# The head of a hybrid streaming-encoder layer: first modulation in four groups of two channel blocks, x transposed in six banks

## What is computed

```python
c_act = jax.nn.silu(c)
mod = (c_act @ w_mod[l] + b_mod[l])[:, None, :]
sh_m, sc_m, gt_m, sh_f, sc_f, gt_f = jnp.split(mod, N_MOD, axis=-1)
h = rms_norm(x, g_pre_mix[l]) * (1.0 + sc_m) + sh_m
y = hybrid_mixer(h, w_in[l], ...)          # begins with proj = h @ w_in, 1024 x 7168
x = x + gt_m * rms_norm(y, g_post_mix[l])
h = rms_norm(x, g_pre_mlp[l]) * (1.0 + sc_f) + sh_f
y = sq_relu_mlp(h, w_mlp_up[l], w_mlp_down[l])
x = x + gt_f * rms_norm(y, g_post_mlp[l])
```

## Time and profile before

| | us |
|---|---|
| median of three executions | 836.4 |
| lowest, highest | 834.62, 836.66 |
| the profiled execution | 835.04 |
| its span in the profile | 833.3 |
| PE busy within the span | 813.3 |

### The profile page before, as it was taken

How to read it: one execution, slowest core, us unless ns; L and a number is a source line. 1 busy time by engine, 2 the same in 40 slices (tenths; PEclk the granted TensorE clock), 3 DMA queues, 4 the chain that set the end, 5 groups by cost and what they waited for, 6 DMA issues and landing times.

```text
span 833.3 us, 12458 instructions
## 1 busy us (share of the span) xinstructions
PE 813.3 (98%) x4270; PEld 701.9 (84%) x4270; DVE 507.5 (61%) x682; ACT 440.0 (53%) x650; POOL 28.3 (3%) x24
## 2 busy tenths in 40 slices
PE   6799999999999999999999999999999999999997
PEld 6588888888888888888888899999999888888885
DVE  4746677656685565566675579777777533333335
ACT  6356777766674444444334566676767622333332
POOL 1542000000000000000000000000000000000000
PEclk9899999999999999999999999999999999999999
DMA  9942333326077666667337031333333532223302
GB/s 290 348 130 82 107 108 107 107 82 182 26 210 219 181 197 201 189 177 209 129 101 253 1 101 44 109 102 101 101 101 101 177 101 96 85 96 101 101 0 101
DMA packets 134943, 109.52 MB, mean 131 GB/s; under 512 B 4460, under 2 KB 119300, under 8 KB 134916
## 3 DMA queue, kind: packets, MB, share of 16 engines
q1 hardware_dynamic: 134740, 109.10, 43.8%
q10 hardware_dynamic: 144, 0.04, 0.0%
q0 software_dynamic: 32, 0.02, 0.0%
HBM read 107.04 MB, written 2.10 MB: 131 GB/s over the span
## 4 chain that ended last, share of the span: by engine, by line
PE 97%; DVE 1%; ACT 1%; POOL 0%; issue 0%; DMA 0%; DVEq 0%; ACTq 0%
PE ps L416 32%; PE ps L417 31%; PE ps L418 31%; PE ps L1460 1%; PE ps L1471 0%; PE ps L1607 0%; PE ps L1483 0%; POOL ht_lo L600 0%; ACT xnt L657 0%; ACT ht_hi L659 0%; PE ps L1579 0%; PE ps L1580 0%; PE ps L1491 0%; DMA crows<-in_c_dram 0%; DVE sums L1331 0%
## 5 line engine op out<-in xcount | busy, mean ns | idle before, releaser
L416 PE MATMUL ps<-ht_hi,w_hi 128*128 128x512 f32 x448 | 176.9, 395 | 8.0 <-POOL ht_lo L600 5.2
L417 PE MATMUL ps<-ht_lo,w_hi 128*128 128x512 f32 x448 | 175.8, 392 | 0.0
L418 PE MATMUL ps<-ht_hi,w_lo 128*128 128x512 f32 x448 | 175.6, 392 | 0.0
L1020 DVE TENSOR_TENSOR w_lo<-raw,w_hi 128x1024 fp32r<-128x1024 f32 x100 | 122.0, 1224 | 56.7 <-ACT w_hi L630 54.9
L630 ACT ACTIVATE w_hi<-raw 128x1024 fp32r<-128x1024 f32 x96 | 100.4, 1049 | 33.3 <-PE ps L418 28.7
L416 PEld LDWEIGHTS ps<-ht_hi,w_hi 128*128 128x128 f32 x448 | 84.9, 189 | 27.2 <-issue 9.5
L418 PEld LDWEIGHTS ps<-ht_hi,w_lo 128*128 128x128 f32 x448 | 84.9, 190 | 18.0
L417 PEld LDWEIGHTS ps<-ht_lo,w_hi 128*128 128x128 f32 x448 | 85.1, 190 | 17.5
L416 PE MATMUL ps<-w_hi,hd_hi 128*128 128x512 f32 x256 | 99.6, 389 | 0.0
L417 PE MATMUL ps<-w_lo,hd_hi 128*128 128x512 f32 x256 | 99.6, 389 | 0.0
L418 PE MATMUL ps<-w_hi,hd_lo 128*128 128x512 f32 x256 | 99.6, 389 | 0.0
(11 more groups left out here) (227 smaller groups left out, 1492.9 us busy)
## 6 DMA issues: line engine op xcount, KB each, us to landing
raw<-in_w_in_dram SPq DMA_DIRECT2D x48, 512.0 KB, 4.8
modraw<-in_w_mod_dram SPq DMA_DIRECT2D x32, 512.0 KB, 4.0
raw<-in_w_mlp_down_dram SPq DMA_DIRECT2D x32, 512.0 KB, 3.3
up_raw<-in_w_mlp_up_dram SPq DMA_DIRECT2D x56, 256.0 KB, 3.4
mod_raw<-in_w_mod_dram SPq DMA_DIRECT2D x32, 256.0 KB, 7.0
xs<-in_x_dram SPq DMA_DIRECT2D x8, 512.0 KB, 5.3
raw<-in_w_a_out_dram SPq DMA_DIRECT2D x8, 512.0 KB, 5.4
raw<-in_w_b_out_dram SPq DMA_DIRECT2D x8, 512.0 KB, 5.5
```

What stands on the lines that cost most here:

```text
L416: nc.tensor.matmul(dst, l_hi, r_hi, start=first, stop=False, skip_group_check=chained)
L417: nc.tensor.matmul(dst, l_hi, r_lo, start=False, stop=False, skip_group_check=chained)
L418: return nc.tensor.matmul(dst, l_lo, r_hi, start=False, stop=last, skip_group_check=chained)
L1020: V.tensor_tensor(w_lo[:, slot, :], raw[:, slot, :], f(w_hi[:, slot, :]), ALU.subtract).then_inc(w_lo_ready, 1)
```

## The change

`GROUPS` becomes four pairs, so the first group covers blocks 0 and 1 and needs 2 MB of weights in place of 1 MB. In it PE takes rows 0 to 3 directly (`mod0_direct`, 16 matmuls of one column, between and behind the transposes), and DVE rows 4 to 7 in `ps`; PE adds DVE's sum with the ones vector. x is transposed into six banks; blocks 6 and 7 are transposed behind the others, into banks 4 and 5 once ACT has copied these to `xnt`. ACT modulates blocks 0 and 1 straight out of `ps`. The unread transposes between the tiles go, and 14 come to stand between the columns of group 0 and the first matmul block. The first weights are split per block instead of per group. SP issues all x tiles, then all eleven vector DMAs, then the modulation's chunks with a block's weights between them. ACT loads its tables for sigmoid and root by one-element activations ahead of need. The columns of the next group are made at (1,1), (3,1), (5,1). Every DVE accumulation of a group now stands behind the column step of the group before.

```diff
-    GROUPS = ((0,), (1,), (2, 3), (4, 5), (6, 7))
+    GROUPS = ((0, 1), (2, 3), (4, 5), (6, 7))
+    PE_ROWS = 4
...
-                    if g0 == 0 and m0 > 0:
-                        sp_eng.wait_ge(mod0_sum, 1)
+                    if g0 == 0 and m0 < PE_ROWS:
+                        sp_eng.wait_ge(mod0_rows, m0 + num0)
...
             for t in range(TB):
                 sp_eng.dma_start(xs[:, t, :], x_v[:, t, :]).then_inc(xr_in[t], 16)
-                if t == 0:
-                    load_vectors(sp_eng, vectors[1::2], vec_in)
-            load_mod0_group(0)
+            load_vectors(sp_eng, vectors, vec_in)
+            per_group = len(CHUNKS) // len(GROUPS)
+            for c in range(per_group):
+                load_mod0(c)
             load_first_units(0)
-            load_first_units(1)
...
+            for g in range(1, len(GROUPS)):
+                for i in range(per_group):
+                    load_mod0(g * per_group + i)
+                    if i == 1:
+                        load_first_units(GROUPS[g - 1][1])
+                    if i == 2:
+                        load_first_units(GROUPS[g][0])
+            load_first_units(NB - 1)
...
             first_units_lo(0)
             pool.wait_ge(h_lo, 1)
+            input_lo(1)
+            first_units_lo(1)
             for g in range(1, len(GROUPS)):
-                first_units_lo(g)
-                for k in GROUPS[g]:
-                    input_lo(k)
+                k0, k1 = GROUPS[g]
+                first_units_lo(k0)
+                input_lo(k0)
+                input_lo(k1)
+                first_units_lo(k1)
...
-            load_vectors(act, vectors[0::2], vec_in)
+            act.wait_ge(const_ready, 4)
+            A(ysum[:, 3 * TB - 1:3 * TB], eps_t[:, 0:1], ACT.Sigmoid)
             act.wait_ge(c_sum, 1)
             A(c_act[:, :], ps[:, B_T0, 0:NB], ACT.Sigmoid).then_inc(sig_c, 1)
+            A(ysum[:, 3 * TB - 2:3 * TB - 1], eps_t[:, 0:1], ACT.Sqrt)
...
-            act.wait_ge(x_tr, NB)
-            for k in (NB - 1, NB - 2, 0, 1, 2):
-                if k == 1:
-                    first_units_hi(0)
+            act.wait_ge(x_tr, X_BANKS)
+            for k in (4, 5, 2):
                 A(xnt[:, k, :], ps[:, k, :], ACT.Copy).then_inc(xnt_ready, 1)
-            act.wait_ge(xnt_ready, 5)
-            modulate(0, 0)
+            first_units_hi(0)
+            for k in GROUPS[0]:
+                modulate(k, 0)
+            first_units_hi(1)
...
-            accumulate(0, range(NB // 2))
-            dve.wait_ge(x_tr, NB)
-            for k in (3, 4, 5):
-                V.tensor_copy(xnt[:, k, :], ps[:, k, :]).then_inc(xnt_ready_dve, 1)
+            accumulate(0, range(PE_ROWS, NB))
+            dve.wait_ge(x_tr, X_BANKS)
+            V.tensor_copy(xnt[:, 3, :], ps[:, 3, :]).then_inc(xnt_ready_dve, 1)
             dve.wait_ge(cols_ready, 2)
             modulation_columns(0)
-            dve.wait_ge(xnt_ready, 2)
-            accumulate(1, range(0, 2))
+            dve.wait_ge(x_tr, NB - 1)
+            V.tensor_copy(xnt[:, 6, :], ps[:, X_LATE[6], :]).then_inc(xnt_ready_dve, 1)
             dve.wait_ge(h_hi, 1)
             V.tensor_tensor(ht_lo[:, 0, :], xnt[:, 0, :], f(ht_hi[:, 0, :]), ALU.subtract).then_inc(h_lo, 1)
-            accumulate(1, range(2, NB))
+            dve.wait_ge(x_tr, NB)
+            V.tensor_copy(xnt[:, 7, :], ps[:, X_LATE[7], :]).then_inc(xnt_ready_dve, 1)
             for g in range(1, len(GROUPS)):
-                if g + 1 < len(GROUPS):
-                    dve.wait_ge(mod0_acc, acc_count(g, NB - 1))
-                    accumulate(g + 1, range(0, 1))
+                accumulate(g, range(NB))
                 modulation_columns(g)
-                if g + 1 < len(GROUPS):
-                    accumulate(g + 1, range(1, NB))
...
+            def mod0_direct(blocks):
+                for m in blocks:
+                    c = CHUNK_OF[0, m]
+                    if m == CHUNKS[c][1]:
+                        pe.wait_ge(mod0_in[c], 32)
+                    for a in range(2):
+                        for k in GROUPS[0]:
+                            last = nc.tensor.matmul(ps[:, B_T1, a * NB + k:a * NB + k + 1],
+                                                    chunk_view(c)[:, m - CHUNKS[c][1], a, k * P:(k + 1) * P],
+                                                    c_act[:, m:m + 1], start=m + a + k == 0, stop=False, skip_group_check=True)
+                    last.then_inc(mod0_rows, 1)
...
-            COLUMNS_AT = {(0, 5): 1, (1, 5): 2, (3, 1): 3, (5, 1): 4}
+            COLUMNS_AT = {(1, 1): 1, (3, 1): 2, (5, 1): 3}
...
+                    if k == 0 and i == 1:
+                        pe.wait_ge(h_f32, 2)
+                    if k == 0 and i >= 3:
+                        pe.wait_ge(xnt_ready_dve, i - 2)
```

More of the change, by code:

```diff
@@ L250, in hybrid_layer_kernel @@
         xnt_ready_dve = sem("xnt_ready_dve")
+        mod0_rows = sem("mod0_rows")
         mod0_acc = sem("mod0_acc")
@@ L1067, in accumulate @@
                         dve.wait_ge(mod0_in[c % M0_BUFS], 32 * (c // M0_BUFS + 1))
[L1068 to L1069 removed]
+                    if m == (PE_ROWS if g == 0 else 0):
+                        V.tensor_scalar(acc, part, c_act[:, m:m + 1], None, ALU.mult).then_inc(mod0_acc, 1)
                     else:
@@ L1456, in _, with unread, mod0_columns @@
             nc.tensor.transpose(ps[:, B_T0, 0:NB], crows[:, :], ident[0:NB, 0:NB]).then_inc(c_sum, 1)
-            def unread(count):
+            def unread(count, dst):
                 for _ in range(count):
-                    nc.tensor.transpose(ps[:, NB // 2, (TB - 1) * P:], ident[:, :], ident[:, :])
-            unread(24)
-            pe.wait_ge(vec_in, 16 * len(vectors))
-            nc.tensor.transpose(ps[:, B_T1, 0:NCOL], vrows[0:NCOL, :], ident[0:NCOL, 0:NCOL]).then_inc(cols_sum, 1)
+                    nc.tensor.transpose(dst, ident[:, :], ident[:, :])
+            def mod0_direct(blocks):
[9 more added lines that the diff above has]
+                    last.then_inc(mod0_rows, 1)
+            def mod0_columns(g):
+                pe.wait_ge(mod0_acc, acc_count(g, NB - 1))
+                for k in GROUPS[g]:
+                    for a in range(2):
+                        last = nc.tensor.matmul(ps[:, B_T1, a * NB + k:a * NB + k + 1], mod0[:, a, k * P:(k + 1) * P],
+                                                ones[:, 0:1], start=g > 0, stop=True, skip_group_check=True)
+                last.then_inc(mod0_sum, 1)
+            last_tokens = ps[:, X_BANKS - 1, (TB - 1) * P:]
+            unread(24, last_tokens)
             pe.wait_ge(cact, 1)
@@ L1467, in _ @@
                 pe.wait_ge(x_norm, t + 1)
-                for k in range(NB):
-                    if t == 0 and k == B_T1:
-                        pe.wait_ge(cols_ready, 1)
+                for k in range(X_BANKS):
                     last = nc.tensor.transpose(ps[:, k, t * P:(t + 1) * P], xs[:, t, k * P:(k + 1) * P], ident[:, :])
@@ L1473, in _ @@
                         last.then_inc(x_tr, 1)
[L1474 to L1495 removed]
+                if t == 0:
+                    pe.wait_ge(vec_in, 16 * len(vectors))
+                    nc.tensor.transpose(ps[:, B_T0, P:P + NCOL], vrows[0:NCOL, :], ident[0:NCOL, 0:NCOL]).then_inc(cols_sum, 1)
+                if t == 1:
+                    mod0_direct(range(0, 2))
+            mod0_direct(range(2, PE_ROWS))
+            for k, late in X_LATE.items():
+                pe.wait_ge(xnt_ready, late - 3)
+                for t in range(TB):
+                    last = nc.tensor.transpose(ps[:, late, t * P:(t + 1) * P], xs[:, t, k * P:(k + 1) * P], ident[:, :])
+                last.then_inc(x_tr, 1)
             pe.wait_ge(const_ready, 3)
             mod0_columns(0)
[L1498 to L1501 removed]
+            pe.wait_ge(xnt_ready, 3)
+            unread(14, ps[:, 2, 0:P])
+            COLUMNS_AT = {(1, 1): 1, (3, 1): 2, (5, 1): 3}
             for k in range(NB):
[L1503 to L1504 removed]
+                pe.wait_ge(w0_lo_ready, k + 1)
                 pe.wait_ge(h_lo, k + 1)
```

98 lines of the change are left out of this document (33 added, 65 removed).

## The result

| | before | after |
|---|---|---|
| median, us | 836.4 | 840.54 |
| lowest, highest | 834.62, 836.66 | 838.71, 842.32 |
| the profiled execution | 835.04 | 840.54 |
| its span | 833.3 | 838.7 |
| mean granted clock in it | 0.992 | 0.987 |

Each kernel was executed five times. The ratio after to before is 1.0058, with a 95% interval of [1.0037, 1.0078]. The forecast of 827.7 and its range up to 831.7 were wrong, in size and in sign.

What follows compares the result with a forecast made beforehand. PE, busy 98%, was taken as the bound: the first block would end at 20.1 + 38.3 = 58.4 against 66.43, 8.0 us less, giving 827.0 from the profiled execution or 828.4 from the median; 827.7 was taken, range 825.0 to 831.7.

Steps and rivals of the forecast that it cites:

- cost nothing as long as x's own 2.1 MB cover them: In the head: moving the eleven vector loads to SP, 3.6 us of issue ahead of the modulation, costs no time.
- rival of a late vector: In the head: a late vector or chunk stops PE; 832.4 us, or 829.5 with half the delay; chance 8%.
- S: Start of the first matmul block, forecast at 20.1 us, bounds 19.4 to 22.0.
- S + 38.3: Forecast end of the first matmul block, counted from its start S; 58.4 us against 66.43 before.
- The data of group 0: In the head: x, vectors and the first group's weights, 4.26 MB, are in at 14.7 us, bounds 13.7 to 15.2.
- rows 6 and 7, 0.81 us each: In the head: once the data are in, DVE does these two rows and is done at 16.3 us.
- since with the clock at full the sum closes: In the head: the reason given for keeping S at 20.1 us, within bounds of 19.4 to 22.0.
- The rival had the right places: Clock falls ahead of the block (1.5 us) or after (1,1) (nine matmuls, 1.8 us); 829.2 to 831.0 us; chance 30%.
- The 0.22 us of a transpose at half clock: In PE's head: 20 transposes at half clock would add 2.2 us, up to 1.5 to 1.9 on S.
- 0.8 ... 0.94 of slack, so nothing: Hand-over behind the block: ACT and DVE come 0.8 us later against PE, within 0.94 of slack at `g_lo`, costing nothing.
- given back behind the block: Hand-over slack is used up and DVE trails PE in the next units; 833 to 836 us; chance 5%.
- slower: Clock stays at half through the block; gain gone from 40 of 144 matmuls, 55 give 838 us; chance 4%.

Runs made afterwards that it cites:

- a2: The changed kernel with the vectors issued as before, five on SP behind x tile 0 and six on ACT; 835.8 us, ratio 1.0001.
- c3: c1 with DVE's first row of pair 2-3 put ahead of block 0's low part; 831.03 us, ratio 0.9932.
- d3: c3 with 14 unread transposes in front of the columns at (1,1); 833.28 us, ratio 0.9952.
- c2: c1 with 34 unread transposes ahead of the first x tile in place of 24; 832.65 us, ratio 0.996.
- d1: c3 with six unread transposes behind each of tiles 0 to 2 and each of the first two direct rows; 832.16 us, ratio 0.996.
- d2: d4 with d1's unread transposes in the head; 831.77 us, ratio 0.9955.
- a1: The changed kernel with POOL's memset of modb two units later; 833.15 us, ratio 0.9944.
- c4: The changed kernel with its last softplus steps written in two-tensor form, four for three, memset in place; 836.06 us, ratio 0.9981.
- c1: The changed kernel with both a1's later memset and a2's vector order; 831.26 us, ratio 0.9927.
- d4: a2 with c3's row, d3's filling and the softplus moved ahead of the columns of pair 4-5; 831.35 us, ratio 0.9945.

## Why the prediction was wrong

**The vectors (step: "cost nothing as long as x's own 2.1 MB cover them").** Wrong, and its rival of a late vector, given 8%, is what happened: the last vector released PE at 11.46. I counted bytes (0.06 MB) and issue time (3.6 us beside x), not what eleven small transfers do to the queues: 270 GB/s where a2 had 357, and a first chunk issued at 6.8 where a2 had 4.3. No run separates these two. The block began 4.9 us later than forecast; 3.5 of it is this (a2: 21.54). Of the 3.5, 1.1 is the vectors' transpose itself (11.46 against 10.39); the other 2.4 came up between it and the ones matmuls (9.77 us against 7.33), where after is at half clock from 12.0 to 18.5 and a2 only to 12.3. By the rival's own sum the end of the block would be S + 38.3 = 63.3.

**The data of group 0 (14.7, and "rows 6 and 7, 0.81 us each").** Mis-sized even without the vectors: in a2 DVE starts its four rows at 13.89 and has them done at 17.1, not 16.3. The third chunk was late and DVE had all four rows still to do, not two. In c3 the columns ended at 18.23 (17.21 + 1.02), not 17.2, and the block began 2.87 later, 2.9 forecast: so rows and columns are the last microsecond of S (21.10).

**The clock ("since with the clock at full the sum closes").** The rival had the right places, ahead of the block and behind (1,1), but in after the stretch behind (1,1) holds 15 matmuls, not nine: 3.0 us, which is about the difference between S + 38.3 and 66.33 - 25.04 = 41.3. In d3, where it does not fall, the block ends 38.1 behind its start (21.46 to 59.5, against 58.4 forecast; the end is the gates' 65.95 less the wait and the 5.61 that one unit takes in after, 71.94 - 66.33). So the chain of the block was right and the price of the clock was not. The 0.22 us of a transpose at half clock was read from a stretch whose granted clock stands as 1.00 in the earlier trace rows; the value itself holds, as 12 transposes took 2.59 us (15.83 to 18.42) at half clock in after. On the transposes, full clock was granted through 60 instructions of the head, more than half of them transposes, in c2's window from 13 to 20 us. The Trainium skill (TensorE: Matmul & The Clock Gate, PE-mode transpose) says that they do not count as busy for the clock; this trace, like the earlier trace rows, disagrees. It is not settled: d1 fell to half at 20.3 us behind 11 us of transposes and one-column matmuls without a pause, and d2, with the same instructions on PE at the same times to 0.01 us from 9.08 to 20.2, did not.

**The hand-over ("0.8 ... 0.94 of slack, so nothing").** The step that decided the sign. I took the slack at `g_lo`, at the end of DVE's chain, and a shift of 0.8 as fitting into it. The shift was mis-sized, and the slack that counted was another. DVE's last softplus steps did come later against the memset, by 1.8 us (67.04 - 66.56 is 0.48 behind its start, 65.31 - 66.65 was 1.34 ahead; 1.07 of it is the longer `w_lo` beside POOL's own, 3.69 against 2.62). That carried the one-tensor steps over the start of a POOL instruction, and the first of them was held for the memset's whole rest. The margin of order was 0.93 us, that of `k_neg`: the forecast shift of 0.8 would have stayed within it, and without the 1.07 of `w_lo` the shift would have been 0.75. So the cause of the crossing is POOL's own `w_lo`, which the change moved behind `ht_lo` to 59.26 and into DVE's; this is worked out from the rows and was not tried alone. None of these rows was in my list. The rival "given back behind the block" has the time, 833 to 836 and more, and got 5%; its mechanism (DVE trails PE) is half of this one. The outcome, slower, got 4%, by half clock throughout the block; after had it there for 7.4 of 41.3 us (25.0 to 25.6 and 32.5 to 39.3).

**What held.** DVE's eight rows end at S + 6.85 (31.89), 7.0 forecast; the wait at (1,1) was 1.58 and 1.69 to 1.87 in a2, c2 and c3, 2.2 forecast; PE never waited for POOL's `w_lo`; from one pair's columns to the next (44.34 to 53.65) 9.31, 9.27 forecast; the tables loaded early. None was worth anything once 5 us were lost ahead of the block.

**The sum.** Forecast 8.0 gained; measured 5.5 lost, a gap of 13.5. The start of the block is 4.9 of it, the clock within it 3.0, the wait for the gates 3.8 and the clock behind that 1.7: 13.4. What is shown by a kernel with that part alone: 3.5 of the start (a2), and 4.4 of the 5.5 at the gates (a1, and 4.3 in c4). Taken singly they need not add up, since the clock in the head is not the same from one execution to the next: after to a1 is 7.4 by the medians, after to a2 4.7, after to c1 (both) 9.3.

**What stays open.** Why the same kernel is granted full clock in the head in one execution and half in the next (829.7 to 835.1 in c1). The traces of the eight kernels with early vectors and no edit ahead of tile 0 but c2's show where it begins. The first 24 unread transposes take 5.38 us if all are 0.22 apart, and less if the pace rises to 0.11 before they are through; when it does differs. They took 4.15, 4.22 and 4.51 us in a2, d3 and c1; PE then waited 2.16 to 2.46 us for tile 0, and the clock fell at 8.9 to 9.3. They took 4.83 to 5.38 in c3, d1, d2 and d4 (5.29 for 34 in c2), the wait was 1.01 to 1.79, and the clock stayed full there. That is eight executions side by side and no test: no run set the wait alone. The later falls, d1's at 20.3 against none in d2, are not explained by it. The filling narrowed the spread in d2, over seven executions, and not in d1 and d3. And of the 0.8 us left at the gates, which d4 lost together with the softplus, the part that is `w_lo` beside POOL's was not tried alone.
